# Modulation turned round: condition columns held in the array, weights streamed past them

## The reference, cut to what matters

```
mod   = silu(c)     @ w_mod + b_mod      # w_mod is 1024 x 6144
mod_c = silu(c_ctx) @ w_mod + b_mod
sh1, sc1, g1, sh2, sc2, g2 = split(mod, 6)
...
hx = rmsnorm(x, norm1_w) * (1 + sc1) + sh1
```

## Time and profile before

| | |
|---|---|
| median of three runs | 3593.56 us |
| span of the profiled execution | 3590.3 us |
| TensorE (PE) busy | 3425.8 us, 95%, 13706 matmuls |
| VectorE (DVE) busy | 2429.7 us, 68% |
| ScalarE (ACT) busy | 1686.0 us, 47% |
| GpSimd (POOL) busy | 472.6 us, 13% |
| TensorE clock granted, mean | 0.971 |
| DMA over the span | 172 GB/s |

### The profile page before, as it was taken

How to read it: one execution, slowest core, us unless ns; L and a number is a source line. 1 busy time by engine, 2 the same in 40 slices (tenths; PEclk the granted TensorE clock), 3 DMA queues, 4 the chain that set the end, 5 groups by cost and what they waited for, 6 DMA issues and landing times.

```text
span 3590.3 us, 43795 instructions
## 1 busy us (share of the span) xinstructions
PE 3425.8 (95%) x13706; PEld 2379.6 (66%) x13706; DVE 2429.7 (68%) x2965; ACT 1686.0 (47%) x2233; POOL 472.6 (13%) x624
## 2 busy tenths in 40 slices
PE   8989999999989999998998999989999999999997
PEld 3344588874344588875654664477788888888885
DVE  4665554453565564455555993279999999999996
ACT  2333332232333332233221123168888888888884
POOL 0000000000000000000000000043343433434331
PEclk9988999999988999999999999999999999999999
DMA  5110333332110233332111003279999999999995
GB/s 189 47 36 24 94 112 118 112 106 71 47 36 24 92 114 117 112 116 72 47 59 59 24 24 100 65 284 354 356 370 361 373 365 363 377 356 373 364 368 210
DMA packets 167984, 618.33 MB, mean 172 GB/s; under 512 B 18528, under 2 KB 18656, under 8 KB 167296
## 3 DMA queue, kind: packets, MB, share of 16 engines
q1 hardware_dynamic: 157200, 573.84, 45.0%
q0 software_dynamic: 10672, 43.00, 4.2%
HBM read 587.92 MB, written 28.84 MB: 172 GB/s over the span
## 4 chain that ended last, share of the span: by engine, by line
PE 81%; DVE 11%; issue 3%; ACT 3%; DMA 1%; POOL 0%; DVEq 0%; ACTq 0%; POOLq 0%; SPq 0%
PE bank L592 54%; PE bank L1134 24%; DVE w_part L2501 2%; DMA sb_ring<-in_w 1%; DVE sb_rstd L1746 1%; DVE sb_work L1788 1%; PE bank L1124 1%; PE bank L1085 1%; PE bank L1142 1%; DVE sb_work L1941 0%; DVE sb_work L2257 0%; DVE sb_work L2301 0%; DVE sb_work L2534 0%; PE bank L913 0%; DVE sb_work L2529 0%
## 5 line engine op out<-in xcount | busy, mean ns | idle before, releaser
L2501 DVE TENSOR_TENSOR w_part<-sb_ring,w_part 128x1024 fp32r<-128x1024 f32 x762 | 889.2, 1226 | 58.8 <-ACT w_part L1650 43.7
L1650 ACT ACTIVATE w_part<-sb_ring 128x1024 fp32r<-128x1024 f32 x762 | 771.3, 1053 | 77.4 <-PE bank L1134 44.0
L1134 PE MATMUL bank<-w_part,xg_hi 128*128 128x512 f32 x2048 | 564.0, 397 | 0.0
L592 PE MATMUL bank<-h_hi,split_part 128*128 128x512 f32 x1408 | 444.9, 400 | 4.7 <-ACT h_hi L1418 4.7
L1134 PEld LDWEIGHTS bank<-w_part,xg_hi 128*128 128x128 f32 x2048 | 383.0, 188 | 89.2
L592 PE MATMUL bank<-sb_work,sb_ring 128*128 128x512 f32 (+5 forms) x880 | 331.6, 531 | 4.0 <-ACT sb_probe L1215 2.6
L1134 PE MATMUL bank<-w_part,xg_lo 128*128 128x512 f32 x1024 | 321.1, 395 | 0.0
L592 PEld LDWEIGHTS bank<-h_hi,split_part 128*128 128x128 f32 x1408 | 265.3, 190 | 68.4 <-ACT h_hi L1418 5.1
L1134 PE MATMUL bank<-w_part,act_hi 128*128 128x512 f32 x1024 | 284.8, 400 | 1.3 <-DVE act_lo L2544 0.6
L592 PE MATMUL bank<-sb_hT,sb_ring 128*128 128x512 f32 (+1 forms) x608 | 274.0, 608 | 8.2 <-ACT sb_hT L1234 8.2
L592 PE MATMUL bank<-h_lo,split_part 128*128 128x512 f32 x704 | 272.2, 393 | 0.0
(11 more groups left out here) (354 smaller groups left out, 4603.5 us busy)
## 6 DMA issues: line engine op xcount, KB each, us to landing
sb_ring<-in_w SPq DMA_DIRECT2D x768, 512.0 KB, 7.4
sb_ring<-in_wstream SPq DMA_DIRECT2D x304, 512.0 KB, 3.6
y_rows<-sb_padc POOLq DMA_DIRECT2D x1, 4096.0 KB, 16.1
sb_xT<-in_x SPq DMA_DIRECT2D x4, 512.0 KB, 7.3
x_rows<-sb_padc SPq DMA_DIRECT2D x1, 2048.0 KB, 9.8
residual<-sb_hT POOLq DMA_DIRECT2D x1, 2048.0 KB, 6.5
sb_hT<-residual POOLq DMA_DIRECT2D x1, 2048.0 KB, 8.1
x_rows<-sb_work SPq DMA_DIRECT2D x1, 2048.0 KB, 6.6
```

Of the source, the lines that this page charges most:

```text
L592: ins = nc.tensor.matmul(out, l, r, start=start, stop=stop)
L1134: ins = nc.tensor.matmul(out[n][:], l[:, k, :], r[:, n * 512:(n + 1) * 512], start=False, stop=(k, p) == (KD - 1, 2))
L1650: nc.scalar.activation(w_hi[t % SPLITS], ring[:, t % RING, :], ACT.Copy).then_inc(s_hi, 1)
L2501: nc.vector.tensor_tensor(w_lo[t % SPLITS], ring[:, t % RING, :], w_hi[t % SPLITS].bitcast(F32), ALU.subtract).then_inc(s_lo, 1)
```

## The change

The modulation matmul is turned round. A chunk is four weight tiles. For each k the two condition columns are now the stationary operand, and the k-th blocks of four tiles move past it as one operand 512 wide. The eight k are dealt to four groups of output partitions (0, 32, 64, 96), so that k and k + 4 accumulate in one group. If the four tiles wrap around the end of the ring, the chunk is done in two pieces of fewer columns. ScalarE copies the bank out to `mod_rows`, TensorE turns it back with four transposes, VectorE sums the four groups and adds the bias. There are twelve chunks: per layer one after ln1's variance and five behind FFN steps 7, 16, 25, 34 and 43; the transposes come behind step 3 and three steps after each of those. GLA and ln2 hold no modulation any more.

```diff
--- before.py
+++ after.py
@@ -265,6 +265,7 @@
                                                 offset=x_at + 4 * (KD * T + i * TILE))[:] for i in range(4)]
         split_hi, split_lo = split_parts[0::2], split_parts[1::2]
         y = xT
+        mod_rows = rows(2)
 
         place[0] = 0
         xtok = rows(TB, SSD_W)
@@ -611,19 +612,32 @@
                 state["stream"] += 1
                 return loaded(state["stream"] - 1)
 
-            def modulation(part):
-
-                out = bank("mod", part)
-                first, n = MOD_PARTS[part]
-                assert state["mod"] == first
+            def modulation(c):
+
+                out = bank("mod_rows", c)
                 pe.wait_ge(act_done, when("csil"))
-                for m in range(n):
-                    w = loaded(MOD_AT + first + m).rearrange("p (k m) -> p k m", m=P)
+                first = state["tile"] % RING
+                for j in range(4):
+                    loaded(MOD_AT + 4 * c + j)
+                whole = min(4, RING - first)
+                for at, slot, n in ((0, first, whole), (whole, 0, 4 - whole)):
+                    if n == 0:
+                        continue
                     for k in range(KD):
-                        mm(out[:, 2 * m:2 * m + 2], w[:, k, :], csil[:, 2 * k:2 * k + 2], k == 0, k == KD - 1,
-                           *(("mod", part) if (m, k) == (n - 1, KD - 1) else ()))
-                    used()
-                state["mod"] += n
+                        j = k % 4
+                        mm(out[32 * j:32 * j + 2, at * P:(at + n) * P].rearrange("p (i m) -> p i m", m=P),
+                           csil[:, 2 * k:2 * k + 2], ring[:, slot:slot + n, k * P:(k + 1) * P], k < 4, k >= 4,
+                           *(("mod_rows", c) if (at + n, k) == (4, KD - 1) else ()))
+                used(4)
+                state["mod"] += 1
+
+            def modulation_turned(c):
+
+                pe.wait_ge(act_done, when("mod_rows_kept", c))
+                out = bank("mod", c)
+                for i in range(4):
+                    ins = nc.tensor.transpose(out[:, i * P:(i + 1) * P], mod_rows[:, c % 2, i * P:(i + 1) * P], ident)
+                ins.then_inc(pe_done, did.up(("full", "mod", c)))
 
             def used(n=1):
                 state["pending"] += n
@@ -645,12 +659,10 @@
                 if center and tag[0] == "cfm":
                     pe.wait_ge(dve_done, when("norm_in", tag))
                     chunks(("mean", tag), lambda k: ones, lambda k: src[:, k, :], n)
-                if ("mean", tag) in MOD_PARTS:
-                    modulation(("mean", tag))
                 chunks(("var", tag), lambda k: ones, lambda k: squares(width)[:, at + k, :], n, width=width,
                        ready=("square", tag))
-                if ("var", tag) in MOD_PARTS:
-                    modulation(("var", tag))
+                if ("var", tag) in MOD_AT_SPOT:
+                    modulation(MOD_AT_SPOT["var", tag])
 
             def running(kind, tag, src, k, ready):
 
@@ -779,8 +791,6 @@
                                True, True, "goff", l, j, h)
                     if j == 0:
                         token_values(l, 2)
-                    if j == 1:
-                        modulation(("gla", l))
                     if j >= 2:
                         project(l, ("gg0", "gg1")[j - 2])
                 pe.wait_ge(dve_done, when("amat", l))
@@ -885,8 +895,10 @@
                         up(t, a, b)
                     if kind == "down":
                         down(t, a, b)
-                    if t in MOD_BEHIND:
-                        modulation(("ff", l, t))
+                    if (l, t) in MOD_AT_SPOT:
+                        modulation(MOD_AT_SPOT[l, t])
+                    if (l, t) in MOD_TURNED_AT:
+                        modulation_turned(MOD_TURNED_AT[l, t])
                     if kind == "down":
                         if a == FFN_PARTS - 1 and b > 0:
                             running("mean", ("ln2", l), xT, b - 1, ("norm_in", ("ln2", l)))
@@ -899,7 +911,7 @@
                 norm(("ln2", l), xT, 0, KD, ones_d)
 
 
-            assert state["mod"] == 6 * KD
+            assert state["mod"] == MOD_CHUNKS
             for k in range(KD):
                 running("var", ("x1",), sq, k, ("square", ("x1",)))
 
@@ -1434,9 +1446,19 @@
                     nc.scalar.activation(act_hi_ff[:, c % ACT_SLOTS, :], gbuf[:, c % 2, :], ACT.Copy).then_inc(act_done,
                         did.up(("act_hi_ff", l, c)))
 
+                def keep_mod_rows(c):
+
+                    act.wait_ge(pe_done, when("full", "mod_rows", c))
+                    if c >= 2:
+                        act.wait_ge(pe_done, when("full", "mod", c - 2))
+                    nc.scalar.activation(mod_rows[:, c % 2, :], bank_of("mod_rows", c)[:], ACT.Copy).then_inc(act_done,
+                        did.up(("mod_rows_kept", c), ("free", "mod_rows", c)))
+
                 for t, (kind, c, v) in enumerate(FFN_SEQ):
                     if 1 <= t < len(FFN_SEQ) - 2:
                         round_tile_ff(t + 2)
+                    if (l, t + 1) in MOD_TURNED_AT:
+                        keep_mod_rows(MOD_TURNED_AT[l, t + 1])
                     if l == DEPTH - 1 and (kind, c) == ("down", FFN_PARTS - 1):
                         if v == CTX_VAR - 1:
                             act.wait_ge(s_ctx, 16)
@@ -1728,14 +1750,15 @@
             norms = []
 
 
-            def modulated(part):
-
-                first, n = MOD_PARTS[part]
-                dve.wait_ge(pe_done, when("full", "mod", part))
-                nc.vector.tensor_tensor(modv[:, first:first + n, :],
-                    bank_of("mod", part)[:, 0:2 * n].rearrange("p (m c) -> p m c", c=2),
-                    col2("b_mod", first, n).unsqueeze(2).to_broadcast([P, n, 2]), ALU.add).then_inc(dve_done,
-                    did.up(("free", "mod", part)))
+            def modulated(c):
+
+                out = modv[:, 4 * c:4 * c + 4, :]
+                dve.wait_ge(pe_done, when("full", "mod", c))
+                nc.vector.tensor_reduce(out, bank_of("mod", c)[:].rearrange("p (i j r) -> p i r j", j=4, r=32)[:, :,
+                    0:2, :], AX, ALU.add).then_inc(dve_done, did.up(("free", "mod", c)))
+                dve.wait_ge(dve_done, did.n)
+                nc.vector.tensor_tensor(out, out, col2("b_mod", 4 * c, 4).unsqueeze(2).to_broadcast([P, 4, 2]),
+                    ALU.add).then_inc(dve_done, did.up())
 
             def inverse(tag, width=T, out=None):
 
@@ -1757,15 +1780,11 @@
 
             def scaled(tag, dst, src, n, gcol, at=None):
 
-                if ("mean", tag) in MOD_PARTS:
-                    modulated(("mean", tag))
                 inv = inverse(tag, out=at)
                 for k in range(n):
                     nc.vector.scalar_tensor_tensor(out=dst[:, k, :], in0=src[:, k, :], scalar=gcol(k), in1=inv,
                         op0=ALU.mult, op1=ALU.mult).then_inc(dve_done, did.up(("normed", tag, k), *([("normed_all",
                         tag)] if k == n - 1 else [])))
-                if ("var", tag) in MOD_PARTS:
-                    modulated(("var", tag))
 
             def rms_scaled(tag, dst, src, gain, width=T):
                 inv = inverse(tag, width)
@@ -2001,8 +2020,6 @@
                             nc.vector.tensor_tensor(qhat[:, d, j % 2, t0:t1], qhat[:, d, j % 2, t0:t1], proj[:,
                                 SLOT["q"], t0:t1], ALU.mult).then_inc(dve_done, did.up(("qhat", l, j, d)))
 
-                    if j == 2:
-                        modulated(("gla", l))
                     if j == 0:
                         centre(("cfm", l), proj, 2)
                     if j in (1, 2):
@@ -2120,8 +2137,8 @@
                 for t, (kind, a, b) in enumerate(FFN_SEQ):
                     if 1 <= t < len(FFN_SEQ) - 2:
                         rest_of_tile_ff(t + 2)
-                    if t - 2 in MOD_BEHIND:
-                        modulated(("ff", l, t - 2))
+                    if (l, t - 2) in MOD_TURNED_AT:
+                        modulated(MOD_TURNED_AT[l, t - 2])
                     if l == DEPTH - 1 and (kind, a, b) == ("down", FFN_PARTS - 1, CTX_VAR + 2):
                         for i, (section, which, name) in enumerate(((1, 1, "norm1_w"), (1, 0, "norm1_w"), (4, 0, "norm2_w"))):
                             dve.wait_ge(dve_done, did.n)
@@ -2585,7 +2602,6 @@
 
 
 MOD_AT = DEPTH * (len(PROJ) + 4 + KD + 2 * KF + -(-KF // 8) * KD)
-MOD_PARTS = {}
 FFN_PARTS = -(-KF // 8)
 FFN_SEQ = []
 for _p in range(FFN_PARTS):
@@ -2594,23 +2610,19 @@
     FFN_SEQ += [("down", _p, _m) for _m in range(KD)]
 
 
-MOD_BEHIND = tuple(range(2, 56, 3))
+MOD_BEHIND = (7, 16, 25, 34, 43)
 MIX_OPEN = 6
 
 
-def _mod_parts():
-    spots = []
-    for l in range(DEPTH):
-        spots += [(("gla", l), 2)]
-        spots += [(("var", ("ln1", l)), 2)] + [(("ff", l, t), 1) for t in MOD_BEHIND] + [(("var", ("ln2", l)), 2)]
-    first = 0
```

(16 more changed lines are left out.)

## The result

| us | median | runs | kernel before, same chip | ratio, 95% interval |
|---|---|---|---|---|
| changed kernel | 3552.20 | 3548.65 to 3555.62 | 3592.84 | 0.9882 (0.9868 to 0.9896) |
| again | 3556.75 | 3555.37 to 3560.38 | 3593.91 | 0.9894 (0.9877 to 0.9910) |
| a third time | 3556.11 | 3548.86 to 3560.82 | 3593.45 | 0.9891 (0.9870 to 0.9911) |

The change makes the kernel faster by 1.0 to 1.2%: 40.6, 37.2 and 37.3 us between the medians. (The ratio on record is not the plain quotient of the medians, which is 0.9887, 0.9897 and 0.9896; either way the gain is clear of the interval.) The forecast was 35.2 us.

The account below looks back on a forecast made before the run. TensorE was taken to bound the FFNs. Span 3590.3 - 61.2 (tiles) + 20.8 (chunks) + 5.2 (transposes) = 3555.1 us; from the median, 3593.6 - 35.2 = 3558.4 us, range 3551 to 3579.

Parts of the forecast that it names:

- some 3 us for where the clock happens to rise after each idle stretch: Allowance at the bounds of the range for TensorE's clock after idle stretches; not a term of the sum.
- What bounds the kernel: In the FFNs TensorE: a microsecond taken off it is one off the kernel, until another engine becomes late.
- The removed tiles, 36 x 1.70: In the FFNs, 18 two-column modulation tiles per layer at 1.70 us each leave the path: 61.2 us.
- The twelve tiles taken as free: Tiles in the GLA and after ln1 and ln2 cost nothing, as TensorE waits there anyway; counted 0.
- The chunk, 2.08 us: Four groups side by side, 1.72 us plus 0.36 for switches; ten in the FFNs cost 20.8 us; chance 0.67.
- The two rival counts of groups: Two at a time: 3.79 us a chunk, 3575.5 us, chance 0.17. In a row: 7.2 us, 3612 us, chance 0.08.
- The transposes, 0.109 us each: Four for each of twelve chunks, all in the FFNs, add 5.2 us.
- ScalarE, VectorE, loads at nothing: The bank copies, group sums and weight loads around the chunks stay covered by TensorE's work; cost 0.
- The rival, 3 us lost behind each chunk: Each FFN chunk leaves 6 us at half clock; ten cost 30 us, 3588 us; chance 0.05 together with buffers.
- The range: 3551 to 3579 us for the whole kernel, taking in two groups at a time with the same 3 us.
- the likeliest case: Four at a time, with free switches (3.6 us less), the GLA's 0.3 us and some 3 us of clock: 3551 to 3563.

Follow-up runs that it names:

- before_moved: Kernel before, with the eight modulation tiles of GLA and ln2 moved behind four more FFN steps per layer; 3615.08 us, ratio 1.0062.
- busy_gla: Changed kernel with five useless float32 matmuls filling the gap behind GLA step 1; 3553.35 us, ratio 0.9892.
- combined: Changed kernel with busy_gla's useless matmuls, one chunk per layer at ln2 and 18 useless transposes at the last chunk but one; 3548.29 us, ratio 0.9878.

## Why the forecast came near, and the step that failed

The forecast was 35.2 us and the first comparison gave 40.6. The mechanism was right; what failed is the step that added it up. The sum has terms for the FFNs alone. All the rest, the clock and the stages that the change doesn't touch, stands in it at nothing, as "some 3 us for where the clock happens to rise after each idle stretch" at the bounds. The runs showed terms of a size in its place: the front of the second block is 2.9 us shorter, because TensorE's clock is lower for less of it, and each FFN pays 1.54 us of clock at the wait for the activations. One term of the sum was mis-sized besides, the removed tiles at 1.70 us each, which measured 1.78. And the expert stage scatters by 11 us from one profile of a kernel to the next, for which the prediction has no term. Step by step:

- **What bounds the kernel.** Right: the time taken off TensorE in the FFN came out of the span whole, and neither ScalarE, VectorE nor a load came late behind a chunk. 17.64 and 17.66 us against "about 17.5 us shorter each".
- **The removed tiles, 36 x 1.70.** Small miss. A tile costs 1.78, so 64.1 us rather than 61.2: the span from its own start to the next start doesn't see that the following matmul is late as well.
- **The twelve tiles taken as free.** Right, by before_moved and by the longer idle times in the GLA and at ln1.
- **The chunk, 2.08 us.** Right: 2.02, four groups side by side. The reasoning, that halves stream at full pace and that four row groups start together, carried over to four column groups of 128 rows each. The two rival counts of groups cost, built by themselves, 3.72 and 7.15 us a chunk (3.79 and 7.2 in the prediction), and the kernels came out at 3576.8 and 3614.1 us against 3575.5 and 3612.
- **The transposes, 0.109 us each.** Right: 0.44 us per four.
- **ScalarE, VectorE, loads at nothing.** Right, by the waits that are left.
- **The clock.** The rival, 3 us lost behind each chunk, is false: 0.99 over the FFNs, as before, and 1.00 over the chunks. But the 3 us at the bounds hold three terms that belong in the sum: +1.54 us in each FFN at the wait for the activations, and -2.9 in the front. The balance of an FFN closes with the first: -18 x 1.78 + 5 x 2.02 + 6 x 0.44 + 1.54 = -17.8 us, measured -17.65. That the sum of 35.2 fits the FFNs' 35.3 so well is thus luck in part: two errors, 2.9 us of tiles and 3.1 us of clock, cancel.
- **The range.** Its low end was too near. The first comparison's 40.6 us are 35.3 (FFNs) and 2.9 (front), less 0.6 (between), and some 3 us of scatter, most likely of the experts, where one and the same program takes 1188 to 1199 us. The prediction allowed 3 us below for the clock and nothing for that stage. Against the other two comparisons, 37.2 and 37.3, the forecast is 2 us off. The upper end of the likeliest case, 3563, doesn't come out of its terms either, which give 3558.4 + 3 = 3561.4.

What stays open: what decides whether the clock falls at a given place of the front, which no run here took apart, and why the loads of the expert stage come at a slightly different rate from one execution to the next.

## What to carry to other kernels

Where a product has only a few stationary or moving columns, keep these in the array and stream the wide operand past them, with the contraction dealt to four groups of output partitions: four products of 128 rows each then take the time of one. Price such fillers from the start of the matmul before to the pace after, on both sides of the change, and build one and two groups as well: the three points show at once what is streaming and what is overhead. Read a change of one per cent by stretches between fixed instructions, and repeat the profile; a stretch that the change doesn't touch can move by 6 us for a shift of 0.7, and then says nothing about the change. When it does, lay its instructions side by side and read the granted clock where they drift apart.

## What the runs showed that was not expected

- The eleven profiles of the changed kernel and its variants fall into two bands, a front of 717.9 to 718.2 us in six and of 723.8 to 724.2 us in five, with nothing between (the kernels with the modulation as before stand between, at 719.6 and 721.0); within one kernel it repeats to 0.03 us. This effect of the clock isn't noise: it comes with the program.
- A wait of 2.84 us at the same place leaves the clock at 1.00 in one program (before, busy_gla) and at 0.86, in the window read there, in the next; in combined it is 0.86 in layer 1 and 1.00 in layer 2.
- 3.5 times from four column groups with all ends counted, into a single bank, in both orders tried (k % 4 and k // 2).
- The expert stage of one program differs by 11 us from one profile to the next on one core.
